# Layer 1's modulation in the first FFN: column strips on TensorE in place of partial sums on VectorE

## The reference

```python
cs = jax.nn.silu(c)
for l in range(DEPTH):
    mod = cs @ P['w_mod'][l] + P['b_mod'][l]
    sh1, sc1, g1, sh2, sc2, g2 = jnp.split(mod[:, None, :], 6, axis=-1)
    hn = _rms_norm(x, P['norm_mix_g'][l]) * (1.0 + sc1) + sh1
    ...
    x = x + g1 * y
    hn = _rms_norm(x, P['norm_ffn_g'][l]) * (1.0 + sc2) + sh2
    x = x + g2 * _swiglu(hn, P['w_ffn_in'][l], P['w_ffn_out'][l])
```

## Time and profile before

| | before |
|---|---|
| median of 3 runs | 1739.27 us (1730.98 to 1742.51) |
| the profiled execution | 1739.32 us |
| its span, first to last instruction | 1737.8 us |
| TensorE matmuls busy | 1535.6 us, 88% |
| VectorE busy | 920.9 us, 53% |
| mean granted TensorE clock | 0.914 of full speed |

### The profile page before, as it was taken

One profiled execution on the slowest core, in us unless ns is written; L12 is line 12 of the kernel. 1 busy time (PEld: TensorE's weight loads), 2 busy tenths in 40 slices (PEclk: granted clock), 3 DMA queues, 4 the chain that ended last, 5 costly groups with the idle time before them and its releaser, 6 DMA issues.

```text
span 1737.8 us, 30106 instructions
## 1 busy us (share of the span) xinstructions
PE 1535.6 (88%) x11068; PEld 1446.1 (83%) x11068; DVE 920.9 (53%) x1670; ACT 518.4 (30%) x780; POOL 128.3 (7%) x148
## 2 busy tenths in 40 slices
PE   6798798796998999999859798888797999999997
PEld 5687687696998999999848686666697999999997
DVE  3745535547874588468673544443446333333344
ACT  3132432423221222122343333332323222222233
POOL 0000000001220021011000000000000000110000
PEclk8599999998998999999969897776798999999999
DMA  8233333242553355344202111111021332223222
GB/s 278 88 116 97 96 109 97 88 133 85 157 157 109 97 159 156 114 125 148 76 0 75 39 38 34 34 33 33 28 84 49 89 92 85 85 84 97 83 72 80
DMA packets 228558, 160.72 MB, mean 92 GB/s; under 512 B 9802, under 2 KB 216348, under 8 KB 228380
## 3 DMA queue, kind: packets, MB, share of 16 engines
q1 hardware_dynamic: 215916, 115.11, 22.5%
q0 software_dynamic: 12288, 44.85, 7.7%
q10 hardware_dynamic: 304, 0.10, 0.0%
HBM read 156.47 MB, written 3.57 MB: 92 GB/s over the span
## 4 chain that ended last, share of the span: by engine, by line
PE 70%; DVE 14%; issue 8%; ACT 5%; DMA 1%; DVEq 1%; ACTq 0%; SPq 0%; POOL 0%; POOLq 0%
PE ring L575 55%; DVE param_rows L472 3%; PE core_j L439 2%; PE core_j L496 2%; DVE weight_low L416 1%; ACT weight_high L411 1%; PE core_j L787 1%; PE core_j L515 1%; PE core_k L792 1%; DVE normed_low L667 1%; PE core_k L1249 1%; PE ring L1226 1%; PE core_k L1166 1%; DMA mixer_area<-in_x_sample 1%; DVE mixer_area L935 1%
## 5 line engine op out<-in xcount | busy, mean ns | idle before, releaser
L575 PE MATMUL ring<-normed_high,weight_high 128*128 128x272 f32 x2128 | 461.9, 299 | 67.8 <-DVE normed_low L667 29.7
L575 PE MATMUL ring<-normed_high,weight_low 128*128 128x272 f32 x2128 | 450.9, 294 | 0.0
L575 PE MATMUL ring<-normed_low,weight_high 128*128 128x272 f32 x2128 | 450.6, 294 | 0.0
L575 PEld LDWEIGHTS ring<-normed_high,weight_high 128*128 128x128 f32 x2128 | 346.4, 196 | 79.0 <-issue 45.7
L575 PEld LDWEIGHTS ring<-normed_low,weight_high 128*128 128x128 f32 x2128 | 346.4, 195 | 0.0
L575 PEld LDWEIGHTS ring<-normed_high,weight_low 128*128 128x128 f32 x2128 | 343.9, 195 | 0.0
L416 DVE TENSOR_TENSOR weight_low<-weight_raw,weight_high 128x1024 fp32r<-128x1024 f32 x197 | 255.6, 1299 | 71.9 <-ACT weight_high L411 68.9
L411 ACT ACTIVATE weight_high<-weight_raw 128x1024 fp32r<-128x1024 f32 x197 | 206.3, 1050 | 176.6 <-PE ring L575 164.6
L575 PE MATMUL ring<-mixed_high,weight_high 128*128 128x272 f32 x960 | 205.2, 296 | 14.4 <-DVE weight_low L416 8.7
L575 PE MATMUL ring<-mixed_high,weight_low 128*128 128x272 f32 x960 | 202.2, 293 | 0.0
L575 PE MATMUL ring<-mixed_low,weight_high 128*128 128x272 f32 x960 | 202.0, 293 | 0.0
(11 more groups left out here) (380 smaller groups left out, 1374.0 us busy)
## 6 DMA issues: line engine op xcount, KB each, us to landing
weight_raw<-in_w_ffn_in SPq DMA_DIRECT2D x88, 512.0 KB, 3.7
mod_weight<-in_w_mod POOLq DMA_DIRECT2D x48, 512.0 KB, 4.1
mod_weight<-in_w_mod POOLq DMA_DIRECT2D x18, 1024.0 KB, 5.4
weight_raw<-in_w_ffn_out SPq DMA_DIRECT2D x32, 512.0 KB, 3.4
weight_raw<-in_a_w_in SPq DMA_DIRECT2D x24, 512.0 KB, 3.7
weight_raw<-in_c_w_in SPq DMA_DIRECT2D x20, 512.0 KB, 3.6
mixer_area<-in_w_mod SPq DMA_DIRECT2D x6, 1024.0 KB, 12.0
weight_raw<-in_w_ffn_out SPq DMA_DIRECT2D x16, 384.0 KB, 3.0
```

What stands on the lines that cost most here:

```text
L575: last = pe.matmul(PS[p.slot][:, half, 0:HALF], w[n.slot][:, k, :], x[:, k, half * HALF:(half + 1) * HALF], start=(k == 0 and w is WH and ...
```

## The change

Layer 1's groups are made as layer 0's are. In the first FFN each `mod_group` becomes `mod_next`, each set of `mod_parts` becomes one `mod_copy`, and the load in halves becomes one load of the whole group behind `low_tile`. The first group's load and strips move ahead, into the output projection of layer 0's mixer. `mod_parts`, `mod_group`, `load_half` and `load_next` go.

```diff
         def out0_pe(pe):
...
-                mod_next(pe, i + 20, not end)
-
-            with pe.Fori(0, KD // 2 - 1) as i:
+                mod_next(pe, i + 20)
+
+            with pe.Fori(0, KD // 2) as i:
                 step(i)
-            step(KD // 2 - 1, True)
...
         def ffn_pe(pe, w0, p0, glo, group, q):
...
                     project(pe, Turn(w, 0, 2, i), Turn(p, 0, 2, i))
                     if group is not None:
-                        mod_group(pe, i + (g - 1))
+                        mod_next(pe, i + (g - 1))
                     project(pe, Turn(w, 1, 2, i), Turn(p, 1, 2, i))
                 if group is not None and a == 0:
-                    mod_group(pe, g + n - 1)
+                    mod_next(pe, g + n - 1)
...
                 if group is not None and a:
-                    mod_group(pe, g + n - 1)
+                    mod_next(pe, g + n - 1, g + n < MOD_TILES)
...
-        def load_next(pool, n, half):
-
-            pool.wait_ge(s_part, n * 16 + 8 * (half + 1))
+        def next_group(pool, l, g):
+
+            pool.wait_ge(s_mrows, g + MOD_TILES // 2 * l - MG_NORM)
             pool.sem_inc(s_note, 1)
-            load_half(pool, lambda: n + 1, half)
+            load_mod(pool, l, lambda: g)
 
         def ffn_pool(pool, gah, mods):
...
                 with pool.Fori(0, n - 1 if end else n) as i:
-                    if mods:
-                        load_next(pool, i + g, 0)
                     low_tile(pool, i, i + gah + a)
                     if mods:
-                        load_next(pool, i + g, 1)
+                        next_group(pool, 1, i + (g + 1))
                 if mods and a == 0:
                     with pool.Fori(0, 2) as i:
-                        for half in range(2):
-                            load_next(pool, i + g + n, half)
+                        next_group(pool, 1, i + (g + n + 1))
...
         def ffn_dve(dve, w0, p0, done, gate, q, group, last=False):
...
                     if mods and not first:
                         mod_read(dve, i + (g - 1))
-                    if mods:
-                        mod_parts(dve, i + g, 0)
+                        mod_copy(dve, i + g)
                     lo_of(dve, Turn(w, 2, 2, i))
-                    if mods:
-                        mod_parts(dve, i + g, 1)
...
-            pool.wait_ge(s_modu, MOD_TILES // 2 - MG_DIRECT)
-            for half in range(2):
-                load_half(pool, lambda: 0, half)
+                next_group(pool, 0, g)
+            next_group(pool, 1, 0)
             ffn_pool(pool, KD, True)
```

More of the change, by code:

```diff
@@ L182, in encoder @@
         ROWS = sb("param_rows", [P, 4, P])
-        ACC = ROWS[:, :, :].rearrange("p (c m) n -> p c (m n)", c=2)
         COLS = sb("param_columns", [P, MOD_ROWS + R1_ALL + R2_ALL])
@@ L313, in encoder @@
         s_mw = sem("mod_weight_in")
-        s_mwh = [sem(f"mod_half_in{s}") for s in range(2)]
         s_early = [sem(f"early_mod_weight_in{s}") for s in range(EARLY_BUFS)]
@@ L320, in encoder @@
         s_mrows, s_mrc = sem("mod_rows_product"), sem("mod_rows_copied")
-        s_part, s_glf = sem("mod_part_step"), sem("hidden_low_done")
+        s_glf = sem("hidden_low_done")
         s_tr = sem("transposed")
@@ L450, in load_mod @@
                            ).then_inc(s_mw, 16)
[L452 to L474, removed]
         def early_parts(dve, g):
@@ L503, in mod_whole @@
             mod_direct(pe, MW, dst).then_inc(s_modu, 1)
[L505 to L508, removed]
         def mod_rows(pe, g):
@@ L749, in out_pe, with step @@
                 if group is not None:
-                    mod_group(pe, group + i)
+                    mod_next(pe, group + i)
         def out0_pe(pe):
             pe.wait_ge(s_glo, KD - 1)
-            def step(i, end=False):
+            def step(i):
                 for j in range(2):
                     project(pe, Turn(W_OUT0, j, 2, i), Turn(R_OUT0, j, 2, i), KD, (GH, GL), mixed=(s_glo, KD))
-                mod_next(pe, i + 20, not end)
-            with pe.Fori(0, KD // 2 - 1) as i:
+                mod_next(pe, i + 20)
+            with pe.Fori(0, KD // 2) as i:
                 step(i)
-            step(KD // 2 - 1, True)
         def ffn_pe(pe, w0, p0, glo, group, q):
@@ L952, in step @@
                         add_square(dve, q, i * size + j, j % 2)
-                    if size == 4:
-                        mod_parts(dve, group + i, j)
                 if group is not None:
                     mod_read(dve, group + i)
+                    mod_copy(dve, group + 1 + i)
             with dve.Fori(0, n) as i:
@@ L971, in step @@
                 mod_read(dve, i + 20)
-                if not end:
-                    mod_copy(dve, i + 21)
+                mod_copy(dve, i + 21)
             with dve.Fori(0, KD // 2 - 1) as i:
@@ L987, in step @@
                         lo_of(dve, Turn(w, 1, 2, i))
-                    if mods and not first:
-                        mod_parts(dve, i + (g - 1), 3)
                     dve.wait_ge(s_fth, i + done + a + 1)
@@ L1004, in step @@
                                              op0=ALU.mult, op1=ALU.mult).then_inc(s_free[ui.slot], 1)
-                    if mods:
-                        mod_parts(dve, i + g, 2)
                 step(0, True)
@@ L1010, in ffn_dve @@
                     step(i)
[L1011 to L1014, removed]
+                if mods and a == 0:
+                    mod_read(dve, g + n - 1)
+                    mod_copy(dve, g + n)
                 end = a == parts[-1][0]
@@ L1020, in ffn_dve @@
                     mod_read(dve, g + n - 1)
+                    if g + n < MOD_TILES:
+                        mod_copy(dve, g + n)
         CW = t["c_w_in"][0].rearrange("(k p) m -> p k m", p=P)
@@ L1837, in _ @@
             with pool.Fori(MG_NORM + 1, MOD_TILES // 2) as g:
-                pool.wait_ge(s_mrows, g - MG_NORM)
-                pool.sem_inc(s_note, 1)
-                load_mod(pool, 0, lambda: g)
-            pool.wait_ge(s_modu, MOD_TILES // 2 - MG_DIRECT)
-            for half in range(2):
-                load_half(pool, lambda: 0, half)
+                next_group(pool, 0, g)
+            next_group(pool, 1, 0)
             ffn_pool(pool, KD, True)
```

## The result

The changed kernel takes 1835.64 us (median of 4 runs, 1819.82 to 1842.26), the one before 1740.6 (4 runs, 1730.98 to 1742.51): a ratio of 1.0545, with an interval of 1.0466 to 1.0623. It is slower, as forecast, and 9 us above the 1827 predicted.

A forecast was written before the change was run, and what follows sets the result against it. The first FFN was taken as bound by TensorE, which stops for modulation groups. 403.4 + 36.5 + 93.6 + 1.7 + 11.6 = 546.8 us against 458.9, 87.9 more: 1827 us; forecast 1805 to 1845 (0.58), range 1784 to 1862.

The forecast's parts named there:

- The FFN without modulation: First FFN: without its 24 modulation groups it would take 403.4 us, the groups costing 55.5 us before the change.
- Strips and folds: TensorE, first FFN: 1.56 us for each of 23 groups and one fold alone, 36.5 us in all.
- The rival in which the weights are on time: GpSimd's issue runs ahead of the hidden tile's split, so the load is hidden: FFN 439.9 us, kernel 1720; chance 0.04.
- The stalls: First FFN: TensorE waits for late group weights, 3.4 us in each of 18 steps, 9.2 at the first part's end.
- the first step: First of 19 loop steps: its project already runs at the lower clock, so a stall of 1.7 us, no new fall.
- the issue: GpSimd's issue of the megabyte load behind the hidden tile's subtraction: 0.4 us, between nothing and 0.8.
- the other half megabyte: SyncE's weight tile loading beside the modulation megabyte: adds 0.3 us to its landing, at most 1.3.
- The clock: First FFN: the granted clock falls behind stalls, costing 1.8 us in each of 18 steps and 2.4 at the part's end.
- the clock holds: Rival: the stalls are as worked out but leave the clock alone; FFN 512.0 us, kernel 1792; chance 0.20.
- The loads collide: Rival: SyncE's half megabyte takes its full 1.3 us, a stall of 4.4 with more clock; kernel 1858 us; chance 0.15.
- Half hidden: Rival: a stall of 1 us at most in each step, without the clock; time within 1% of before; chance 0.03.
- what would show it: First FFN: 3.4 us idle before strips in 18 steps, steps near 18.8 us, lower clock; VectorE's busy time about 160 lower.

The follow-up runs named there:

- load-first kernel: Against the changed kernel, GpSimd issues the next group's weights ahead of the hidden tile's subtraction instead of behind it; 1723.95 us, 0.988 of before.
- strips later: Against the changed kernel, strips and fold stand behind the step's second project, VectorE's read and copy at the step's end; 1735.57 us, 0.9937 of before.
- 20 matmuls: The changed kernel plus unread matmuls ahead of the strips, 20 in each loop step, 64 at the first part's end; 1792.23 us, 1.0268 of before.
- the two kernels that hold the load back: Changed kernel, load ahead of the subtraction but held until VectorE has read the second project (1762.11 us, 1.0088) or TensorE has ended it (1743.27 us, 0.9979).
- load halfway: Against the changed kernel, GpSimd's load stands between its wait for the hidden tile's high part and the subtraction; 1810.02 us, 1.0375 of before.
- the load held for VectorE's read: Against the changed kernel, the load is ahead of the subtraction but held until VectorE has read the second project; 1762.11 us, 1.0088 of before.
- the changed kernel and the other five: Besides the changed kernel: load halfway (1810.02 us), layer 1's modulation left out (1689.06), strips later (1735.57), load held for VectorE (1762.11) or TensorE (1743.27).

## Why the prediction was right

The sum over the first FFN was 546.8 us; the window is 551.5. Term by term:

- *The FFN without modulation*: 403.4 forecast from the two FFNs, 405.0 measured.
- *Strips and folds*: 36.5 forecast from layer 0's spacing, 36.3 measured. Together 441.3, the load-first kernel's window. The rival in which the weights are on time was priced at 1720 us; that kernel takes 1723.95.
- *The stalls*: 18 x 3.4 + 1.7 + 9.2 = 72.1 forecast, 60.4 measured: 18 of 2.8 us, 0.5 in the first step, 8.8 at the part's end. The step that failed is the issue, taken as 0.4 behind the subtraction; the load starts 0.06 ahead of its end (676.02 against 674.72 + 1.36). And the other half megabyte, taken as 0.3, is worth about 0.1: the landing is 5.5 in the median, 5.4 before. In the first step, taken as 1.7, the wait was 0.5.
- *The clock*: 18 x 1.8 + 2.4 = 34.8 forecast; 551.5 - 441.3 - 60.4 = 49.8 measured. The step that failed is the 1.8 a step, the mean over six waits of before. One of them had left the clock alone, and it stood for a sixth of the cases; here 17 of the 18 long waits in steps were followed by the lower level. That is the smaller part: the other five alone give 2.1. The falls here also lasted longer. In the 12 us from the strips' start the granted clock is 0.72 or 0.73 in 11 of the 17 steps and 0.86 in six, 3.4 and 1.7 us:

```profile
453.02:465.02 12.00, 12.00 (x79) 11.02 (x80) 2.39 (x4) 0.19 (x1) 0.00 (x0) 0.72 0.23 67
...
895.72:907.72 12.00, 12.00 (x92) 11.42 (x93) 2.53 (x5) 1.61 (x2) 0.84 (x1) 0.86 0.19 57
```

  Of the five of before three stood at 1.7. Why the long falls came more often was not tested. Behind the part's end the window gives 7.17 x 0.39 = 2.8 us, and the 2.9 us of strips and folds ahead of it, at the lower level as well, half of theirs: 4.2 for the 2.4 forecast. That leaves (49.8 - 4.2) / 18 = 2.5 a step; the window of one step above gives 6.89 x 0.33 = 2.3 without its strips. Some 1.7 of the 49.8 are the fall behind the wait at the FFN's start (0.86 over the 12 us from 428.17), which the load-first kernel happened not to have; less these it is 2.4 a step.

So two terms were off, one 11.7 too high and one 15.0 too low, and nearly cancel: the nearness of the time is partly luck. The profiled execution, the slowest of the four at 1842.26, is some 15 us above the forecast: 4.7 of them in the FFN, 10.6 ahead of it and between the two FFNs, where the sum has nothing. The mechanism is shown by the edits: take the late issue away and the loss goes (load first), hide its DMA under a project and it goes (strips later), keep TensorE busy through the stall and the clock's part goes (20 matmuls).

On the rivals: *the clock holds* was priced at 1792, and with TensorE kept busy the kernel takes 1792.23; in the changed kernel itself it doesn't hold. *The loads collide* needed 1.3 us of sharing in the megabyte's landing; about 0.1 was there. The two loads do share: it is SyncE's half megabyte, issued 1.4 us behind the megabyte, that lands late. Its landings from 640 to 700 us in the changed kernel, then from 600 to 700 before:

```profile
weight_raw<-in_w_ffn_in SPq DMA_DIRECT2D x7, 512.0 KB, 5.6
...
weight_raw<-in_w_ffn_in SPq DMA_DIRECT2D x12, 512.0 KB, 3.7
```

No step waits for that tile, so it costs nothing here. *Half hidden* does not happen by itself; the two kernels that hold the load back, with stalls of 0.4 and 1.2 us, show that its price was right, at 0.9979 and 1.0088.

On the Trainium skill, "TensorE: Matmul & The Clock Gate", section "HAM oscillation — how this bites in real kernels", by which a loop that waits for a DMA in every tile starts each turn cold: 17 of 18 steps agree. The loop that this section of the Trainium skill tells of waits about 3 to 5 us in each tile. The kernel with waits of 1.2 us in each step shows that a wait in every turn is not enough: none of its 18 was followed by a fall.

Of what would show it: the stall ahead of the strips, the longer step and the lower clock came. VectorE's fall of "about 160" is 149.2. That line of the forecast took the 158.5 of the earlier trace rows alone: it left out the 24 copies that come in, though I had named them, and the 48 first products of the partial sums, which go as well (first the copies in the changed kernel, then the products before):

```profile
L503 DVE COPY param_rows<-core_j 128x256 f32<-128x256 f32 x24 | 10.2, 423 | 0.0
...
L469 DVE TENSOR_SCALAR param_rows<-mod_weight,silu_c 128x256 f32<-128x256 f32 x48 | 14.9, 352 | 2.8 <-DVE modulation L538 0.3
```

158.5 + 14.9 - 10.2 is 163.2, or 14.0 more than measured. Of that, 5.7 are VectorE's weight splits, which take 261.3 us in the changed kernel and 255.6 before. The rest was not taken apart; groups whose rows overlap in time add up to more than the engine's busy time.

## What to carry to other kernels

Moving work to the engine that bounds a stage can pay if it is cheaper there, but ask first when its operands arrive: here 5.5 us of DMA, issued behind an instruction that itself waits for the end of the step, turned a gain of 17.6 us into a loss of 92.6 in the same stage. In a queue that runs in order, put a prefetch ahead of the waits that it doesn't need. Price a stall of TensorE twice, by its length and by the clock behind it, and price the second from waits of the same length.

## What the runs showed of the hardware

- An issue on GpSimd is not a fixed price. From the release of the wait to the load it took 0.95 us with nothing between them (load halfway) and 0.82 us behind the strips' end (load first, 625.12 to 625.94); behind a running subtraction of 1.36 us it added nothing to the subtraction's end. An instruction taken from in front of a load therefore saved less than its own length (0.6 of 1.36).
- A longer wait was followed by the lower clock level more often, with one wait in each step throughout: none of 18 from 1.05 to 1.74 us (the load held for VectorE's read), 14 of 18 in the kernel with the load halfway (all but one of those waits from 2.05 to 2.35 us), 17 of 18 from 2.7 to 3.4 us in the changed kernel. Behind the one not followed, at 645.67, the granted clock stayed at 1.00, as behind the wait at 833.40 in the earlier trace rows. The length alone does not decide: behind the same wait of 2.25 us near the FFN's start the clock of the next 12 us was 1.00 with the load first and with TensorE kept busy, and 0.86 in the changed kernel and the other five.
- Of two loads in flight together here, the one that started second paid. The megabyte on GpSimd's queue landed in 5.5 us with half a megabyte on SyncE's behind it, 0.1 more than before. SyncE's half megabyte (of `w_ffn_in`), issued 1.4 us later, took 5.5 to 5.9 us in the 16 cases of the changed kernel's first FFN, against 3.7 in the median of the 23 with no load of GpSimd beside them.
